# One inverse level of an RWKV-7 chunk solve moved from TensorE to VectorE, and the steps around it placed anew

## The chip, the cores and the metric

The kernel runs on one core of one Trainium2 chip, in float32 throughout. The metric is the device time of one execution in microseconds, the median of the runs.

## The reference, cut to what matters

One layer of a decoder: RMSNorm, an input projection, RWKV-7 time mixing (16 heads of 64) beside retention (8 heads of 128), an output projection, then a mixture of experts. There are 256 positions of a prompt and 8 short sequences of 8 positions ("the sample"), 320 positions in all. The change touches the RWKV part alone:

```python
def _wkv_step(S, inp):
    r, w, k, v, kk, b = inp
    sa = jnp.einsum('bhvk,bhk->bhv', S, -kk)
    S = S * w[:, :, None, :] + sa[..., :, None] * b[:, :, None, :] + v[..., :, None] * k[:, :, None, :]
    y = jnp.einsum('bhvk,bhk->bhv', S, r)
    return S, y
```

The kernel does not step through positions. It cuts the prompt into four chunks of 64 positions and solves each with matrices: Gram products of the scaled keys (b, k) with the queries (kk, r) give a strictly triangular 64x64 matrix M per head and chunk, and sa for all positions of a chunk follows from the inverse of 1 - M. That inverse is built by doubling: level 0 gives the inverse in blocks of 2, each further level k joins two blocks of size 2^k into one, X <- X + X (M masked to level k) X, up to level 5 (blocks of 64). The sample's matrix (blocks of 8) needs levels 0 to 2.

## The kernel before, in words

The projection weights come in tiles of 1 MB. For each of 8 pairs of RWKV heads (with one retention head beside it) there are seven tiles, in the order k, r, v, q, kr, vr, g. Each tile is a 2048x128 matrix multiplied with the 2048x320 activations by TensorE in 8 parts; a part is four matmul instructions with 320 columns as the trace counts them (line 722). The small work of a pair is cut into named steps. The tables PLAN (lines 71 to 79) and PLAN0 (for the first pair) list, for each tile, which steps follow each of its 8 parts; "|" ends a part, "@k" is the taking over of tile k's result, and a "-" marks a step of the pair before. Every engine walks the same list in order and does its own share of each step, so a step's place in the list is its place in the queue of TensorE, VectorE (DVE), ScalarE (ACT) and GpSimd (POOL) alike. Between engines only semaphores order the work. The first pair is written out, a loop runs over the other seven, and the last steps of the last pair run beside the output projection. Every VectorE instruction waits for the one before it; VectorE's are recorded at line 1432, ScalarE's at 1162, GpSimd's at 1984.

The steps that matter here:

- b2b (VectorE) makes the last operand for the Gram products. my copies the pair before's y out of PSUM; then mu (TensorE L866) sums it and va (L869) sums its squares; p2 is a product on VectorE for a later step.
- g0 to g3 are the Gram products of the four chunks (TensorE L754 and L755, results masked and evicted by VectorE), g4 those of the sample (L757, L758).
- "@v" on VectorE mixes v with its shifted self (three instructions); ScalarE copies the tile out of PSUM first. cv keeps v's last columns (two tiny copies).
- ax (ScalarE): packs the 32x32 diagonal blocks of M of the four chunks, two heads, into one tile Ac (four copies of 32 partitions, "ac"), and the off-diagonal ones for level 5 into A5 (two more).
- am (GpSimd): masks the sample's matrix for levels 1 and 2 (As), and Ac for levels 1 to 4 (Am).
- u0 (VectorE): level 0 of the prompt's inverse, as Vc = Ac * mask + unit; its 32x32 transposes (Uc); and Uc spread into a block-diagonal form (Ud).
- us0 (VectorE): level 0 of the sample's inverse and its transpose Us ("us").
- Level k of the prompt is three steps: k1 to k5 transpose Uc on TensorE (L785), i1 to i5 multiply with the mask of the level (eight small instructions, L795), j1 to j5 multiply both results (eight, L804); ScalarE and VectorE copy the results out between them, and VectorE adds and spreads again.
- zs1 (TensorE L777) and ds1 (L782) are level 1 of the sample, zs2 and ds2 level 2. zs1 needs As and Us.
- r0 to r3, a0 to a3 and s0 to s3 then step through the chunks; VectorE copies r2's result of the pair before early in tile k.

Before the change the order from tile v on was: g4 after part 4 of v; mu and g0 after part 5; g1; g2 and g3 after part 7; then after the parts of q: va, u0 | cv, us0 | | k1, i1 | zs1 | j1, pd | ds1 | k2, i2.

After the pairs come the output projection, a router and the experts, whose 400 MB of weights keep the DMA engines busy until the end.

Of the kernel before, what the change touches and what calls it, by code (L numbers as in the profile page):

```python
# [6 lines left out]
ALU = mybir.AluOpType  # L7
# [3 lines left out]
P = 128  # L11
# [8 lines left out]
NC = TP // C  # L20
NCH = NC + 1
LEVELS = 6
BK, NB32 = 32, 4
INNER = 5
# [82 lines left out]
def build_program(nc, xT, win, w_out, params, lora_mu, shT, lora_w, gmix, cst, head_cst,  # L107
# [3 lines left out]
    with ctx:  # L111
# [34 lines left out]
        ones = sbt(128)  # L146
# [36 lines left out]
        def cut(at, n, **axes):  # L183

            x = inv[:, at:at + n]
            return x.rearrange("p (c n) -> p c n", **axes) if axes else x
# [15 lines left out]
        Vc = cut(3712, 128, c=NC)  # L202
        squares = [x[:, 0:4 * T] for x in (GM.rearrange("p c n -> p (c n)"), tok.rearrange("p a c n -> p (a c n)"), wide4)]
# [89 lines left out]
        def sem(name):  # L293
            if name not in sems:
                sems[name] = ctx.enter_context(nc.semaphore(name))
            return sems[name]
# [22 lines left out]
        def wait_freed(e, step, p):  # L319

            e.wait_ge(free(step), nth(step, p))
# [10 lines left out]
        def done(name):  # L332

            return sem("done_" + name)

        def wait_done(e, name, p):
            e.wait_ge(done(name), p + 1)
# [338 lines left out]
        def _(pe):  # L676
# [11 lines left out]
            pe.wait_ge(sem("ones_set"), 1)  # L688
# [37 lines left out]
            def step(p, s):  # L726
# [43 lines left out]
                elif s in ("zs1", "zs2"):  # L770
                    k = int(s[-1])
                    pe.wait_ge(lmk, (INNER + 1) * p + k)
# [10 lines left out]
                elif s[0] == "k":  # L783
                    pe.wait_ge(inverse, 2 * (INNER * p + int(s[1])) - 1)
                    nc.tensor.transpose(b[:, 0:P], Uc[:, :, :], ident).then_inc(full(s), 1)  # L785
                elif s[0] == "i":
                    k = int(s[1])
                    pe.wait_ge(inverse, 2 * (INNER * p + k))
                    if k < INNER:
                        pe.wait_ge(lmk, (INNER + 1) * p + 2 + k)  # L790
                    else:
                        pe.wait_ge(done("ac"), 2 * p + 2)
# [364 lines left out]
        def _(act):  # L1157
# [62 lines left out]
            def step(p, s):  # L1220
# [33 lines left out]
                elif s == "ax":  # L1254
                    wait_freed(act, "g2", p)
                    wait_freed(act, "g3", p)
                    for q in range(NB32):
                        last = A(Ac[quarter[q], :, :], gcell[quarter[q], :, q % 2, :], ACT.Copy)
                    last.then_inc(done("ac"), 1)
                    for h in range(2):  # L1260
                        last = A(A5[quarter[2 * h], :, :], gcell[quarter[2 * h], :, 1, :], ACT.Copy)
                    last.then_inc(done("ac"), 1)
                elif s in ("k1", "k2", "k3", "k4"):
# [161 lines left out]
        def _(dve):  # L1425
# [23 lines left out]
            swapped = [i ^ 1 for i in range(32)]  # L1449

            FILL(eps[:, 0:1], NORM_EPS)
            FILL(eps[:, 1:2], LNX_EPS).then_inc(sem("eps_set"), 1)
            FILL(ones, 1.0).then_inc(sem("ones_set"), 1)
# [99 lines left out]
            def step(p, s):  # L1553
# [63 lines left out]
                elif s == "u0":  # L1617
                    dve.wait_ge(done("ac"), 2 * p + 1)
                    TT(Vc[:, :, :], Ac[:, :, :], inner[0][:, None, :].broadcast_to([P, NC, BK]), ALU.mult)
                    TT(Vc[:, :, :], Vc[:, :, :], unit[:, None, :].broadcast_to([P, NC, BK]), ALU.add)  # L1620
                    TR(Uc.rearrange("p c j -> p (c j)"), Vc.rearrange("p c j -> p (c j)")).then_inc(inverse, 1)
# [5 lines left out]
                elif s in ("i1", "i2", "i3", "i4"):  # L1627
                    wait_filled(dve, s, p)
                    spread(Zd, bank(s)[:, 0:P].rearrange("p (b j) -> p b j", b=NB32)).then_inc(free(s), 1)
                elif s in ("j1", "j2", "j3", "j4"):  # L1630
# [348 lines left out]
        def _(pool):  # L1979
# [16 lines left out]
            def step(p, s):  # L1996
                if s == "am":
                    wait_freed(pool, "g4", p)
                    for k in range(1, 3):
                        TT(As[:, k - 1, :], GM[:, NC, 0:P], lvlT[k], ALU.mult).then_inc(lmk, 1)  # L2000
                    pool.wait_ge(done("ac"), 2 * p + 1)
                    for k in range(1, INNER):
                        TT(Am[:, k - 1, :, :], Ac[:, :, :], inner[k][:, None, :].broadcast_to([P, NC, BK]), ALU.mult).then_inc(lmk, 1)
# [157 lines left out]
```

## Time and profile before

| | us |
|---|---|
| median of 3 runs | 1880.41 (1880.20 to 1882.89) |
| profiled execution, its own time | 1880.75 |
| span of that execution | 1878.9 |
| TensorE busy in the span | 1549.3 (82%) |
| VectorE busy | 627.8 (33%) |
| ScalarE busy | 275.0 (15%) |
| GpSimd busy | 62.0 (3%) |
| mean granted TensorE clock | 0.911 |

The span runs from the first to the last instruction; the execution's own time has what lies around it as well. The eight pairs take roughly the first half of the span; in it TensorE is busy in nearly every slice and the DMA engines in a third. In the second half it is the other way round: the experts' weights arrive at about 428 GB/s and TensorE waits for them. The mean clock is below 1 because of the second half; in the first it is at its upper level throughout.

### The profile page before, as it was taken

To read this page: it belongs to the slowest core of one execution; us is meant where nothing else is said; L and a number is where in the kernel's file an instruction comes from. 1 tells how busy PE (TensorE), PEld (TensorE's weight loads), DVE (VectorE), ACT (ScalarE), POOL (GpSimd) and SP (SyncE) were. 2 spreads that over 40 slices of the span, in tenths; PEclk is the share of its full clock that TensorE was granted. 3 is DMA by queue.
4 is the path that set the end of the run, shared out by engine and by line. 5 is a ranking of instruction groups with operands and counts; after the bars stand their busy time and mean duration, and the time that the engine had idled before them with its cause. 6 is when DMAs were issued, how large, how long until landed. Compare 5 with 4: busy or idle time off the path is not lost.

```text
span 1878.9 us, 24721 instructions
## 1 busy us (share of the span) xinstructions
PE 1549.3 (82%) x8990; PEld 891.2 (47%) x8990; DVE 627.8 (33%) x1264; ACT 275.0 (15%) x592; POOL 62.0 (3%) x103
## 2 busy tenths in 40 slices
PE   7999999999999999999996675766757667576664
PEld 4676767676767676766662231222312223122111
DVE  6746565656565656420031110111102111020014
ACT  2222222222222222200102000000000000000002
POOL 1000000000000000000000000000000000000000
PEclk9999999999999999999997887878878788787778
DMA  7323232323232323275489999999999999999996
GB/s 283 107 98 108 101 104 100 108 94 113 89 120 83 120 82 120 71 292 203 157 373 426 428 429 428 428 428 429 428 429 428 428 429 428 428 428 429 428 407 252
DMA packets 71904, 510.35 MB, mean 272 GB/s; under 512 B 20496, under 2 KB 23696, under 8 KB 37808
## 3 DMA queue, kind: packets, MB, share of 16 engines
q1 hardware_dynamic: 71808, 509.60, 67.1%
q8 instruction: 29, 0.48, 0.1%
q14 instruction: 19, 0.16, 0.0%
q0 software_dynamic: 48, 0.12, 0.0%
HBM read 499.87 MB, written 9.82 MB: 271 GB/s over the span
## 4 chain that ended last, share of the span: by engine, by line
PE 51%; DMA 34%; DVE 10%; issue 2%; SPq 1%; DVEq 1%; ACT 0%; ACTq 0%
DMA arena<-w_up 22%; PE ps_PJ L722 18%; DMA arena<-w_down 12%; DVE arena L1432 10%; PE ps_C L1079 8%; PE ps_PJ L933 7%; SPq L559 1%; PE ps_C L1130 1%; PE ps_SB L1130 1%; PE ps_YB L1130 1%; PE ps_C L795 1%; PE ps_RT L1130 1%; PE ps_SB L764 1%; PE ps_C L804 1%; PE ps_C L755 1%
## 5 line engine op out<-in xcount | busy, mean ns | idle before, releaser
L722 PE MATMUL ps_PJ<-arena 128*128 128x320 f32 x1792 | 539.8, 437 | 0.0
L1079 PE MATMUL ps_C<-arena 128*32 128x512 f32 x2048 | 286.5, 722 | 178.5 <-DMA arena<-w_gate 112.2
L722 PEld LDWEIGHTS ps_PJ<-arena 128*128 128x128 f32 x1792 | 322.8, 190 | 120.1 <-issue 18.0
L1432 DVE TENSOR_TENSOR arena<-arena,ps_PJ 128x512 f32<-128x512 f32 (+2 forms) x112 | 73.6, 657 | 612.7 <-PE ps_PJ L1033 493.3
L1079 PEld LDWEIGHTS ps_C<-arena 128*32 128x32 f32 x2048 | 79.8, 130 | 378.3 <-issue 375.9
L1432 DVE TENSOR_TENSOR arena<-arena 128x512 f32<-128x512 f32 (+12 forms) x311 | 161.8, 520 | 62.4 <-ACTq L421 26.7
L1162 ACT ACTIVATE arena<-ps_C 128x128 f32<-128x128 f32 (+3 forms) x68 | 27.5, 404 | 919.4 <-PE ps_C L1079 532.4
L933 PE MATMUL ps_PJ<-arena 128*128 128x320 f32 x512 | 142.4, 433 | 1.0 <-DVEq L421 1.0
L1162 ACT ACTIVATE arena<-arena 128x320 f32<-128x320 f32 (+11 forms) x206 | 98.0, 476 | 271.7 <-DVEq L421 87.6
L933 PEld LDWEIGHTS ps_PJ<-arena 128*128 128x128 f32 x512 | 95.5, 190 | 40.2 <-issue 3.3
L1432 DVE TENSOR_TENSOR arena<-ps_PJ,arena 128x512 f32<-128x512 f32 x32 | 22.1, 692 | 257.8 <-PE ps_PJ L1026 257.6
L1130 PE MATMUL ps_C<-arena 128*32 128x512 f32 x224 | 41.4, 818 | 79.3 <-DMA arena<-w_down 78.3
L1033 PE MATMUL ps_PJ<-arena 128*128 128x512 f32 (+1 forms) x192 | 96.4, 621 | 3.5 <-ACTq L421 3.3
L1026 PEld LDWEIGHTS ps_PJ<-arena 128*128 128x128 f32 x768 | 87.0, 192 | 12.6 <-issue 12.6
L1026 PE MATMUL ps_PJ<-arena 128*128 128x128 f32 x768 | 89.9, 277 | 0.0
L1984 POOL TENSOR_TENSOR arena<-arena 128x128 f32<-128x128 f32 (+2 forms) x80 | 55.7, 696 | 703.4 <-DVEq L421 380.5
L1432 DVE SCALAR_TENSOR_TENSOR arena<-arena 128x320 f32<-128x320 f32 (+6 forms) x145 | 72.6, 501 | 15.5 <-DVE arena L1432 10.9
L1033 PEld LDWEIGHTS ps_PJ<-arena 128*128 128x128 f32 (+1 forms) x192 | 26.6, 170 | 72.7 <-DVEq L421 45.4
L1432 DVE TENSOR_TENSOR arena<-ps_C,arena 128x320 f32<-128x320 f32 (+3 forms) x77 | 43.2, 561 | 49.7 <-PE ps_C L795 22.7
L1432 DVE RECIPROCAL arena<-arena 128x320 f32<-128x320 f32 (+1 forms) x29 | 54.6, 1881 | 6.0 <-ACTq L421 2.6
L1162 ACT ACTIVATE arena<-ps_SB 128x512 f32<-128x512 f32 (+4 forms) x80 | 36.4, 455 | 123.9 <-PE ps_SB L764 48.3
L1130 PEld LDWEIGHTS ps_C<-arena 128*32 128x32 f32 x224 | 7.0, 125 | 95.3 <-issue 95.3
(185 smaller groups left out, 1190.8 us busy)
## 6 DMA issues: line engine op xcount, KB each, us to landing
arena<-w_down SPq DMA_DIRECT2D x64, 2048.0 KB, 20.8
arena<-w_gate SPq DMA_DIRECT2D x61, 2048.0 KB, 20.6
arena<-w_up SPq DMA_DIRECT2D x61, 2048.0 KB, 20.3
arena<-win SPq DMA_DIRECT2D x59, 1024.0 KB, 4.8
arena<-w_out SPq DMA_DIRECT2D x16, 1024.0 KB, 7.5
arena<-w_gate SPq DMA_DIRECT2D x6, 1024.0 KB, 8.0
arena<-xT SPq DMA_DIRECT2D x8, 640.0 KB, 8.5
arena<-s_ret SPq DMA_DIRECT2D x8, 512.0 KB, 3.8
```

Of the source, the lines that this page charges most:

```text
L559: sp.dma_start(dst, src).then_inc(ex_in[s], 16)
L722: last = mm(pj(j)[:, 0:T], wt[j % NSLOT][:, kt, :], hT[:, kt, :], start=kt == 0, stop=kt == KT - 1)
L755: mm(b[:, 2 * C:320], Kd_[:, c, :], AR[:, c, 0:192], start=True, stop=True).then_inc(full(s), 1)
L764: last = nc.tensor.transpose(b[:, c * P:(c + 1) * P], src[:, c, :], ident)
L933: last = mm(pj(m)[:, 0:T], w[:, i, :], yT[:, KORD[i], :], start=i == 0, stop=i == KT - 1)
L1026: last = mm(XB[b][:, k * P:(k + 1) * P], x1[:, t, kt * P:(kt + 1) * P], pick[:, t, :], start=t == 0, stop=t == 2)
L1033: mm(XB[b][0:nt, :], gT[:, t0:t0 + nt], yp[:, n * F:(n + 1) * F], start=True, stop=True).then_inc(x_full[b], 1)
L1079: last = mm((GB, UB)[u][h * CAP:(h + 1) * CAP, :], xg[:, kt, h * CAP:(h + 1) * CAP], w[h](k), start=kt == 0, stop=kt == KT - 1)
L1130: last = mm(DB[n][h * CAP:(h + 1) * CAP, :], hhT[:, 2 * k + j, h * CAP:(h + 1) * CAP], w[h][:, j, n * F:(n + 1) * F], start=k + j == 0, st ...
L1162: ins = nc.scalar.activation(*args, **kw)
L1432: ins = build(*args)
L1984: ins = nc.gpsimd.tensor_tensor(*args)
```

## The change

Level 1 of the prompt's inverse is no longer done with k1, i1 and j1. u0 does it on VectorE: with blocks of 2 already inverted, one entry of a row and two columns of a group of four are all that changes, so two shuffles across partitions bring the rows needed into place and five small element-wise steps finish the level, ahead of the transposes. GpSimd makes the level's mask product Am[0] first for it. The four copies of ax that fill Ac are shared: two stay on ScalarE, two go to VectorE at the head of u0, and GpSimd waits for all four before any of its products. The Gram products move back by one part (g4 to part 5 of v, beside mu; g3 to the first part of q), p2 goes ahead of g4, cv ahead of ax and u0, and va stands behind cv. zs1, ds1 and the levels from 2 on keep their places. The banks of PSUM lose the three names, and the counts of the semaphores follow. The two semaphores of the set-up constants become one.

```diff
-    "C0": ["g0", "g3", "i1", "i2", "i3", "i4", "i5", "r0", "r1", "r2", "r3"],
+    "C0": ["g0", "g3", "i2", "i3", "i4", "i5", "r0", "r1", "r2", "r3"],
...
 PLAN = {
     "k": "-@g -u1 -th | -s1 | zw -u2 | -r2 -mr za | pc | -a2 pe | -mg | -s2",
     "r": "@k ck | -r3 | sq p1 | -a3 b1k ss | b1l | ps -s3 | pk | b1 b2a",
-    "v": "@r b2b cr -e3 | | | -my | g4 p2 | -mu g0 | g1 | g2 g3",
-    "q": "@v ax am -va u0 | cv us0 | | k1 i1 | zs1 | j1 pd | ds1 | k2 i2",
+    "v": "@r b2b cr -e3 | | | -my | p2 | g4 -mu | g0 | g1 g2",
+    "q": "@v g3 cv -va | ax am u0 | us0 | | zs1 | pd | ds1 | k2 i2",
...
 PLAN0 = {
-    "v": "@r b2b cr | | mk | | g4 p2 | g0 | g1 | g2 g3",
+    "v": "@r b2b cr | | mk | | g4 p2 | g0 | g1 | g2",
...
+        rows4, pair4 = cut(3584, 128, c=NC), inv[:, 1536:1600].rearrange("p (g e) -> p g e", e=2)
...
                 elif s in ("zs1", "zs2"):
-                    pe.wait_ge(lmk, (INNER + 1) * p + k)
+                    pe.wait_ge(lmk, (INNER + 1) * p + 1 + k)
...
                 elif s == "ax":
                     wait_freed(act, "g2", p)
                     wait_freed(act, "g3", p)
-                    for q in range(NB32):
+                    for q in range(2):
                         last = A(Ac[quarter[q], :, :], gcell[quarter[q], :, q % 2, :], ACT.Copy)
-                    last.then_inc(done("ac"), 1)
+                    last.then_inc(done("packing"), 1)
...
+            third_row = [i // 4 * 4 + 2 for i in range(32)]
+            second_row = [i // 4 * 4 + (1 if i % 4 == 0 else 2) for i in range(32)]
...
                 elif s == "u0":
-                    dve.wait_ge(done("ac"), 2 * p + 1)
+                    CP(Ac[quarter[2], :, :], gcell[quarter[2], :, 0, :])
+                    last = CP(Ac[quarter[3], :, :], gcell[quarter[3], :, 1, :])
+                    dve.wait_ge(done("packing"), 2 * p + 1)
+                    last.then_inc(done("ac"), 1)
                     TT(Vc[:, :, :], Ac[:, :, :], inner[0][:, None, :].broadcast_to([P, NC, BK]), ALU.mult)
                     TT(Vc[:, :, :], Vc[:, :, :], unit[:, None, :].broadcast_to([P, NC, BK]), ALU.add)
+                    x1, v1, sx = by_four(Am[:, 0, :, :]), by_four(Vc), by_four(rows4)
+                    SHUF(rows4[:, :, :], Vc[:, :, :], third_row)
+                    dve.wait_ge(lmk, (INNER + 1) * p + 1)
+                    TT(pair4[:, :, 0:1], x1[:, :, 2:3], sx[:, :, 3:4], ALU.mult)
+                    TT(x1[:, :, 3:4], x1[:, :, 3:4], pair4[:, :, 0:1], ALU.add)
+                    SHUF(rows4[:, :, :], Am[:, 0, :, :], second_row)
+                    TT(pair4[:, :, :], sx[:, :, 2:4], v1[:, :, 1:2].broadcast_to([P, BK, 2]), ALU.mult)
+                    TT(x1[:, :, 2:4], x1[:, :, 2:4], pair4[:, :, :], ALU.add)
+                    TT(Vc[:, :, :], Vc[:, :, :], Am[:, 0, :, :], ALU.add)
                     TR(Uc.rearrange("p c j -> p (c j)"), Vc.rearrange("p c j -> p (c j)")).then_inc(inverse, 1)
                     spread(Ud, Uc).then_inc(inverse, 1)
...
                 if s == "am":
                     wait_freed(pool, "g4", p)
+                    wait_done(pool, "ac", p)
+                    TT(Am[:, 0, :, :], Ac[:, :, :], inner[1][:, None, :].broadcast_to([P, NC, BK]), ALU.mult).then_inc(lmk, 1)
                     for k in range(1, 3):
                         TT(As[:, k - 1, :], GM[:, NC, 0:P], lvlT[k], ALU.mult).then_inc(lmk, 1)
-                    pool.wait_ge(done("ac"), 2 * p + 1)
-                    for k in range(1, INNER):
+                    for k in range(2, INNER):
                         TT(Am[:, k - 1, :, :], Ac[:, :, :], inner[k][:, None, :].broadcast_to([P, NC, BK]), ALU.mult).then_inc(lmk, 1)
```

Of the "for h in range(2)" copies into A5 on ScalarE nothing changes but the name of the semaphore.

## Rows read from the trace of the kernel before

**Rows 1.** The page: busy time, share of the span, instruction count.
```profile
PE 1549.3 (82%) x8990; PEld 891.2 (47%) x8990; DVE 627.8 (33%) x1264; ACT 275.0 (15%) x592; POOL 62.0 (3%) x103
```

**Rows 2.** Stretch of one pair: us, busy (count) by engine, PEclk, DMA share, GB/s.
```profile
432.90:526.20 93.30, 92.51 (x517) 65.46 (x516) 55.01 (x115) 23.50 (x56) 6.96 (x10) 1.00 0.30 102
```

**Rows 3.** Waits, 160 to 850 us, TensorE's weight loads: total us, times, longest.
```profile
PEld ps_SB L777 <- DVEq L421: 3.3, 7, 0.5
```

**Rows 4.** Timeline, TensorE, Gram stretch: start, us, instruction, count [idle before <-releaser].
```profile
427.56 7.70 PE L722 MATMUL ps_PJ<-arena 128*128 128x320 f32 x28
435.87 0.56 PE L757 MATMUL ps_SB<-arena 128*128 128x192 f32 x2 [0.60 <-DVEq L421]
...
436.59 1.24 PE L722 MATMUL ps_PJ<-arena 128*128 128x320 f32 x4
437.86 0.78 PE L866 MATMUL ps_RT<-arena 128*128 128x320 f32 x2
```

**Rows 5.** Timeline, VectorE, start of its chain and the Gram stretch.
```profile
412.43 0.29 DVE L1432 COPY arena<-ps_C 128x128 f32<-128x128 f32 x1 [1.56 <-PE ps_C L816]
...
437.05 0.49 DVE L1432 COPY arena<-ps_YB 128x320 f32<-128x320 f32 x1
...
443.18 0.49 DVE L1432 TENSOR_TENSOR arena<-ps_C,arena 128x320 f32<-128x320 f32 x1 [0.22 <-PE ps_C L755]
```

**Rows 6.** Timeline, TensorE, the first inverse level.
```profile
447.66 0.27 PE L785 MATMUL ps_C<-arena 128*128 128x128 f32 x1
...
448.35 1.34 PE L722 MATMUL ps_PJ<-arena 128*128 128x320 f32 x4
449.67 0.49 PE L777 MATMUL ps_SB<-arena 128*128 128x128 f32 x2
...
451.16 0.43 PE L804 MATMUL ps_C<-arena 128*32 128x128 f32 x8
451.52 1.34 PE L722 MATMUL ps_PJ<-arena 128*128 128x320 f32 x4
452.70 0.38 PE L782 MATMUL ps_SB<-arena 128*128 128x128 f32 x2
```

**Rows 7.** Timeline, VectorE, from the v mix to the sample's inverse.
```profile
444.08 0.40 DVE L1432 TENSOR_SCALAR arena<-arena 128x329 f32<-128x329 f32 x1 [0.41 <-DVE arena L1432]
...
445.65 0.85 DVE L1432 TENSOR_TENSOR arena<-arena 128x128 f32<-128x128 f32 x2 [0.23 <-DVE arena L1432]
...
448.58 0.62 DVE L1432 TENSOR_TENSOR arena<-arena 128x128 f32<-128x128 f32 x2
449.24 0.32 DVE L1432 STREAM_TRANSPOSE arena<-arena 128x128 f32<-128x128 f32 x1
```

**Rows 8.** Timeline, ScalarE, the six packing copies.
```profile
443.76 2.12 ACT L1162 ACTIVATE arena<-arena 32x128 f32<-32x128 f32 x6 [0.77 <-DVEq L421]
```

**Rows 9.** VectorE by form, whole span: busy, mean ns | idle before.
```profile
L1432 DVE STREAM_SHUFFLE arena<-arena 128x320 f32<-128x320 f32 x16 | 8.2, 515 | 0.2
...
L1432 DVE TENSOR_TENSOR arena<-arena 128x32 f32<-128x32 f32 x19 | 3.7, 193 | 0.6
...
L1432 DVE TENSOR_TENSOR arena<-ps_RT,arena 128x64 f32<-128x64 f32 x8 | 1.8, 225 | 0.3
...
L1432 DVE COPY arena<-arena 128x128 f32<-128x128 f32 x1 | 0.2, 226 | 0.0
```

**Rows 10.** Timeline, GpSimd, beside it.
```profile
445.91 0.45 POOL L1984 TENSOR_TENSOR arena<-arena 128x128 f32<-128x128 f32 x1 [0.18 <-POOL arena L1984]
```

**Rows 11.** Stretches around idle TensorE: columns as in rows 2.
```profile
59.90:67.00 7.10, 5.03 (x25) 4.06 (x25) 6.14 (x19) 0.00 (x0) 0.00 (x0) 1.00 0.00 0
1001.00:1003.40 2.40, 0.00 (x0) 0.00 (x0) 2.08 (x4) 0.00 (x0) 0.00 (x0) 1.00 1.01 430
1003.50:1006.90 3.40, 1.85 (x7) 1.34 (x7) 0.69 (x2) 1.04 (x2) 0.00 (x0) 0.50 1.02 434
1047.00:1051.20 4.20, 4.15 (x20) 1.13 (x24) 0.00 (x0) 0.00 (x0) 0.00 (x0) 0.50 1.02 429
```

More of the change, by code:

```diff
@@ L687, in _ @@
             last.then_inc(used, 1)
-            pe.wait_ge(sem("ones_set"), 1)
+            pe.wait_ge(sem("eps_set"), 2)
             pe.wait_ge(win_in[1], 16)
@@ L783, in step @@
                 elif s[0] == "k":
-                    pe.wait_ge(inverse, 2 * (INNER * p + int(s[1])) - 1)
+                    pe.wait_ge(inverse, 2 * ((INNER - 1) * p + int(s[1]) - 1) - 1)
                     nc.tensor.transpose(b[:, 0:P], Uc[:, :, :], ident).then_inc(full(s), 1)
@@ L787, in step @@
                     k = int(s[1])
-                    pe.wait_ge(inverse, 2 * (INNER * p + k))
+                    pe.wait_ge(inverse, 2 * ((INNER - 1) * p + k - 1))
                     if k < INNER:
@@ L791, in step @@
                     else:
-                        pe.wait_ge(done("ac"), 2 * p + 2)
+                        pe.wait_ge(done("packing"), 2 * p + 2)
                     for c in range(NC):
@@ L1256, in step @@
                     wait_freed(act, "g3", p)
-                    for q in range(NB32):
+                    for q in range(2):
                         last = A(Ac[quarter[q], :, :], gcell[quarter[q], :, q % 2, :], ACT.Copy)
-                    last.then_inc(done("ac"), 1)
+                    last.then_inc(done("packing"), 1)
                     for h in range(2):
                         last = A(A5[quarter[2 * h], :, :], gcell[quarter[2 * h], :, 1, :], ACT.Copy)
-                    last.then_inc(done("ac"), 1)
-                elif s in ("k1", "k2", "k3", "k4"):
+                    last.then_inc(done("packing"), 1)
+                elif s in ("k2", "k3", "k4"):
                     wait_filled(act, s, p)
@@ L1449, in _, with by_four @@
             swapped = [i ^ 1 for i in range(32)]
+            third_row = [i // 4 * 4 + 2 for i in range(32)]
+            second_row = [i // 4 * 4 + (1 if i % 4 == 0 else 2) for i in range(32)]
+            def by_four(x):
+                return x.rearrange("p c (g e) -> p (c g) e", e=4)
             FILL(eps[:, 0:1], NORM_EPS)
             FILL(eps[:, 1:2], LNX_EPS).then_inc(sem("eps_set"), 1)
-            FILL(ones, 1.0).then_inc(sem("ones_set"), 1)
+            FILL(ones, 1.0).then_inc(sem("eps_set"), 1)
             dve.nop().then_inc(proj_free, NL)
@@ L1626, in step @@
                     TR(Us, V[:, NC, :]).then_inc(done("us"), 1)
-                elif s in ("i1", "i2", "i3", "i4"):
+                elif s in ("i2", "i3", "i4"):
                     wait_filled(dve, s, p)
                     spread(Zd, bank(s)[:, 0:P].rearrange("p (b j) -> p b j", b=NB32)).then_inc(free(s), 1)
-                elif s in ("j1", "j2", "j3", "j4"):
+                elif s in ("j2", "j3", "j4"):
                     wait_filled(dve, s, p)
```

4 rows, old and new, of the table BANKS are left out of this document.

## The prediction

> **What bounds the kernel now.** I read the page first: TensorE is busy 82% of the span [rows 1], which says little, since stages with different limits are mixed in it. The view by stretch shows one pair of heads: every 93.3 us TensorE is busy 92.5 us at a granted clock of 1.00 (the upper level, 2.4 GHz), VectorE 55 us, the DMA engines 30% [rows 2]. So in the eight pairs a microsecond more or less on TensorE's own path is a microsecond of the kernel, while VectorE's busy share proves nothing: what counts is whether it is late at a point where TensorE waits. The waits of the weight loads name such a point: zs1, the first product of the sample's own inverse (L777), waited for VectorE in seven of seven pairs after the first, up to 0.5 us [rows 3]. The timelines give the other two. After b2b, g4 starts at 435.87, where 28 products of 0.27 us from 427.56 would have let it start at 435.12: 0.75 us late. Then mu is 0.19 late (436.59 and four products make 437.67, it starts at 437.86), because y's copy on VectorE runs from 437.05 to 437.54 [rows 4, 5]. That chain of VectorE hangs on the copy of r2 at 412.43, for which VectorE waited 1.56 us on TensorE [rows 5]; from there to y's copy it has no wait for TensorE above 0.1 us in its timeline. All numbers are of the pair that runs from 432.9 us; the others repeat it within 0.1 us.
>
> **Level 1 leaves TensorE.** k1 and i1 (a transpose, eight small products) stand between 447.66 and 448.35: 0.69. The four projection products after them reach zs1 at 449.67, 1.32 later, where they need 1.08: 0.24 more, part of it zs1's wait. So 0.93 goes before zs1. j1 costs 0.09 before it (449.99 to 451.16 for four products, 449.99 being zs1's 0.32 after 449.67), 0.36 itself and 0.10 after it (451.52 to 452.70): 0.55 goes behind zs1 [rows 6]. If nobody were late, that would be 1.48 us a pair, 11.8 us in all.
>
> **g4 and mu.** g4 goes one projection part (1.08) later, to 436.20, and mu directly behind it. The wait at g4 (0.75) ends, but mu is now reached at 436.92 and y's copy still ends at 437.54: nothing in the k and r tiles changes, the r2 copy is still released by TensorE, and "my" stands ahead of p2 and g4 as before ahead of g4. So mu starts at 437.86 as before and waits 0.94 = 0.75 + 0.19. With g4 and the same projection parts done at that moment, the gain is 0. If the anchor moved earlier, it would be at most 0.94 a pair (7.5 us); if the swap of p2 and g4 slowed mu's own chain, some tenths the other way. I take 0.
>
> From mu on TensorE does the same work in another order: g3 moves behind the first q part, beside va. It is at the point of the old k1 (447.66) within 0.02, then makes one more part of 1.08: it reaches zs1 at 448.76.
>
> **VectorE up to zs1.** It must finish u0 and then us0 (Us), in this order, before zs1. Before: the last Gram product was evicted by 443.67 (443.18 + 0.49), the mix of v, u0, cv and us0 followed, and Us was ready at 449.56 (449.24 + 0.32), 0.11 before zs1 started [rows 5, 6, 7]. There is no slack there. Now the same chain:
> - The last eviction ahead of v's mix is g2's; with g3 gone from this place TensorE is 0.55 (one Gram pair) earlier, so it ends at 443.13. The mix keeps its 1.76 (443.67 to 445.43): 444.89.
> - g3 is evicted now behind it, 0.22 + 0.49 as in its row: 445.60. cv moves ahead of u0, 0.27 + 0.47: 446.34. Both were in the chain before, so up to here only 0.54 of the order is gained and 0.71 given back.
> - Two packing copies. The nearest copy takes 0.23 [rows 9]; with gaps 0.63: 446.97. ScalarE's other two of the six that took 2.12 [rows 8] start when g3 is evicted and need 0.7, so they are done before. Sharing the copies takes 1.4 us off ScalarE's part and puts 0.6 on the chain.
> - u0's old content: 445.43 to the end of its spread at 447.69, 2.26 [rows 7]: 449.23.
> - Its new content: two shuffles, two products and sums of 32 columns, two of 64, one of 128, and a wait for GpSimd's Am1. A shuffle of 320 columns takes 0.515, one of 128 then 0.31 (about 1 ns a column, as between the products of 64 and 32), with mask load and gap 0.37; twice 0.74. 32 columns 0.193 twice; 64 columns 0.225 twice; 128 columns 0.29; five gaps of 0.03; the wait 0.2 as other waits of this chain [rows 7, 9]. Sum 2.22: 451.45.
> - us0's 1.13 (448.43 to 449.56): 452.58. u0's seven two-input steps (two old, five new) run beside GpSimd's six products (Am1 comes first now, the rest follow): two such steps took 0.85 beside GpSimd and 0.62 without it [rows 7, 10]; I add 0.1. Us at 452.7, zs1 at 452.8.
>
> TensorE reaches zs1 at 448.76 and waits 4.0 us. Against 449.67 zs1 is 3.1 late; behind it 0.55 of j1 is saved. **A pair becomes 2.58 us longer.** In pair 0 VectorE is late already (it builds masks there), zs1 hangs on the same chain, and I take 2.4. Sum: 7 x 2.58 + 2.4 = 20.4 us. Nothing gives it back: the whole later part of the pair is shifted, VectorE waits for TensorE at r2 in the next pair, and the output projection and the expert loads begin when TensorE has come so far. Bounds: with every step at its shortest and no gap for the wait zs1 is 0.5 earlier, 17 us in sum (it could not go below nothing: nine steps are added and none taken out); with every two-input step slowed as the pair in rows 7 and 0.3 at each of two waits 0.6 later, 25 us. The respaced i2 to k5 keep their places; the banks C0 to C2 lose one use each; SP's queue issues the same pieces in the same order, and nothing new is queued there.
>
> Two waits are added. VectorE waits for ScalarE's two copies ahead of u0, with us0 behind it: free, as worked out. GpSimd now waits for "ac" before the two masks of the sample (As) too, which zs1 also needs: "ac" comes at 447.0, and three products of 0.45 and their gaps of 0.18 [rows 10] end at 449, before Us; it costs nothing while Us is later, and zs1 would start at 449.1 if VectorE were done.
>
> The Trainium skill ("SBUF — State Buffer", section "Who interferes with whom") says that a VectorE instruction with two SBUF inputs contends with a GpSimd instruction that reads SBUF, and that the one that comes second is blocked for the whole of the other. The 0.85 against 0.62 agrees in sign; by full blocks of 0.45, six of them, a pair would be 2.7 longer still, 22 us in all. The rows show a quarter of that, and I stay with them.
>
> **The clock.** In the pairs it never left 1.00: in pair 0 TensorE stood 2.07 us before g4 (60.0 to 62.1), and the stretch around it is at 1.00. But where it stood from 1001.0 to 1003.9 the clock was 1.00 until 1003.4 and 0.50 (1.2 GHz) in the stretch behind; and when dense work came back at 1047 it ran at 0.50 for 4.2 us, half of which, 2.1, is lost [rows 11]. A wait of 4.0 us once a pair is longer than the one that was followed by a fall and longer than any in the pairs now. In how many of the eight pairs the clock falls the rows don't say: none costs 0, all cost 8 x 2.1 = 17. I take four: 8.4 us.
>
> The Trainium skill ("TensorE: Matmul & The Clock Gate", section "What's actually happening") speaks against the change here: "the default state is throttled, and activity releases the throttle". By that rule all eight pairs would restart at the lower level, and the sum would be 1918.
>
> **Forecast**: on the profiled execution's 1880.75 (span 1878.9 and 1.85 around it) 20.4 + 8.4 make 1909.5; the median of the runs is 0.3 lower, 1909.
>
> **Rivals.**
> - A: the wait comes, the clock holds. For it: 4.0 us stands among 92 us of dense work, and 2.07 did nothing. Time 1880.4 + 20.4 = 1901.
> - B: GpSimd's products and VectorE's block one another fully (from rows, every two-input step as long as the 0.45 product beside it: six times 0.45 a pair), with some clock falls: 1880.4 + 20.4 + 22 + 8 = 1931. Against it: the pair of 0.85.
> - C, faster: VectorE's chain isn't what zs1 waits for, because the copies, shuffles and small steps fall into time in which VectorE idles now (0.9 us before g2's eviction, 0.4 before the mix). Then level 1 pays its 1.48 a pair: 1880.4 - 11.8 = 1868.6. It decides at 0.55: if Us comes less than 0.55 us later than now the pair is shorter, else longer. Against it: the added steps are nine and the smallest such step in the rows takes 0.19, so 1.7 at least, and rows 3 show no slack.
> - D: the pieces balance within 4 us of 1880; it needs the same as C with half the cover.
>
> **Chances.** Forecast (the wait and clock falls in two pairs or more) 0.50, A 0.34, B 0.04, C 0.08, D 0.04. Range: the likeliest and A with their bounds, 1880.4 + 17 - 2 (pair 0 may cost less) to 1880.4 + 25 + 17: 1895 to 1922; above and below it lie B, C, D. No change means within 0.2% (3.8 us), about what a measurement of this kernel can tell: slower 0.88, same 0.04, faster 0.08.
>
> **What will show it.** On the changed kernel's timeline: zs1's weight load waits some 4 us for VectorE in each pair (3 or less would make my VectorE sum wrong, none would make C right); g4 has no wait and mu one of 0.9; the period is 95.9 us plus the clock's share; from the end of the eviction ahead of v's mix to Us it takes 9.6 us (443.13 to 452.7; before 5.9, 443.67 to 449.56); there are stretches at 0.50 in the pairs, none before. The forecast is wrong if the period is below 93.3, or if the clock's share is 0 or above 17 us.

## The result, and the profile after

The changed kernel takes 1919.7 us (median of 5 runs, 1917.9 to 1920.5) against 1880.4: a ratio of 1.0204 (95% interval 1.0193 to 1.0215), slower. The profiled execution took 1919.68 us by its own time.

Its page: the span, TensorE's busy time, and the costliest group of instructions.

```profile
span 1917.9 us, 24456 instructions
...
PE 1559.5 (81%) x8854; PEld 902.9 (47%) x8854; DVE 633.2 (33%) x1328; ACT 267.5 (14%) x568; POOL 60.1 (3%) x103
...
L723 PE MATMUL ps_PJ<-arena 128*128 128x320 f32 x1792 | 552.4, 447 | 0.0
```

TensorE has fewer instructions (8854 against 8990) and is yet busy longer (1559.5 us against 1549.3 in [rows 1]): the 1792 projection products (L723 now, L722 before) take 447 ns each in the records; in the kernel before, the same group had 437. They run slower, and nothing about them was changed.

The stretch of one pair (columns as in [rows 2]) and the waits of TensorE from 60 to 900 us (total, times, longest), which answer to [rows 2, 3]:

```profile
374.80:473.60 98.80, 93.98 (x500) 67.22 (x499) 55.74 (x123) 22.50 (x53) 6.69 (x10) 0.97 0.28 96
```

```profile
PE ps_SB L778 <- DVEq L422: 31.3, 8, 3.9
PE ps_RT L867 <- DVEq L1717: 5.4, 7, 0.9
```

A pair takes 98.8 us here and its clock is 0.97, where it was 93.3 and 1.00. zs1 (L778 now) waits 3.9 us in each of the seven pairs after the first and 3.7 in the first; mu (L867) waits for y's copy in the seven pairs that have one; the wait at g4 is gone but for pair 0.

TensorE's timeline of the same pair, answering to [rows 4, 6]: the products ahead of g4, g4, mu, the four parts ahead of zs1, zs1, and what follows it.

```profile
447.38 8.78 PE L723 MATMUL ps_PJ<-arena 128*128 128x320 f32 x32
455.99 0.49 PE L758 MATMUL ps_SB<-arena 128*128 128x192 f32 x2
456.32 0.49 PE L759 MATMUL ps_SB<-arena 128*128 128x192 f32 x2
457.57 0.78 PE L867 MATMUL ps_RT<-arena 128*128 128x320 f32 x2 [0.76 <-DVEq L1717]
...
464.14 4.47 PE L723 MATMUL ps_PJ<-arena 128*128 128x320 f32 x16
472.56 0.80 PE L778 MATMUL ps_SB<-arena 128*128 128x128 f32 x2 [3.95 <-DVEq L422]
473.15 4.47 PE L723 MATMUL ps_PJ<-arena 128*128 128x320 f32 x8
477.42 0.63 PE L783 MATMUL ps_SB<-arena 128*128 128x128 f32 x2
477.85 1.71 PE L723 MATMUL ps_PJ<-arena 128*128 128x320 f32 x4
```

g4 starts without a wait; mu starts 1.25 after g4's second half, 0.94 later than it could; zs1 starts 14.99 us after mu (forecast 14.94). Then look at the durations: sixteen products of a projection take 4.47 ahead of zs1, and eight take 4.47 behind it.

VectorE's timeline, answering to [rows 5, 7]: the copy of r2, y's copy, the evictions of g1 and g2 (one line), g3's, cv with the two packing copies, and u0 and us0 to the transpose that ends in Us; behind it ScalarE's four copies (two into Ac, two into A5).

```profile
432.23 0.29 DVE L1433 COPY arena<-ps_C 128x128 f32<-128x128 f32 x1 [1.56 <-PE ps_C L817]
...
456.76 0.49 DVE L1433 COPY arena<-ps_YB 128x320 f32<-128x320 f32 x1
...
461.63 1.13 DVE L1433 TENSOR_TENSOR arena<-ps_C,arena 128x320 f32<-128x320 f32 x2 [1.13 <-PE ps_C L756]
...
464.74 0.49 DVE L1433 TENSOR_TENSOR arena<-ps_C,arena 128x320 f32<-128x320 f32 x1 [0.22 <-DVE arena L1433]
465.50 1.09 DVE L1433 COPY arena<-arena 128x1 f32 x4 [0.27 <-DVE arena L1433]
466.84 0.75 DVE L1433 TENSOR_TENSOR arena<-arena 128x128 f32<-128x128 f32 x2 [0.25 <-ACTq L422]
...
467.64 0.30 DVE L1433 STREAM_SHUFFLE arena<-arena 128x128 f32<-128x128 f32 x1
468.08 0.70 DVE L1433 TENSOR_TENSOR arena<-arena 128x32 f32<-128x32 f32 x2
...
469.15 0.99 DVE L1433 TENSOR_TENSOR arena<-arena 128x64 f32<-128x64 f32 x3
...
470.64 1.46 DVE L1433 TENSOR_TENSOR arena<-arena 128x512 f32<-128x512 f32 x3
472.14 0.31 DVE L1433 STREAM_TRANSPOSE arena<-arena 128x128 f32<-128x128 f32 x1
```

```profile
465.32 1.43 ACT L1163 ACTIVATE arena<-arena 32x128 f32<-32x128 f32 x4 [0.45 <-DVEq L422]
```

From the end of g2's eviction (462.76) to Us (472.45) it is 9.69 us; the forecast said 9.6.

The stretches around zs1's wait, by window (columns as in [rows 2]; the granted clock, third from the end, is the point):

```profile
468.70:472.40 3.70, 0.00 (x0) 0.00 (x0) 3.16 (x11) 0.00 (x0) 1.39 (x4) 0.94 0.70 222
472.60:479.20 6.60, 6.60 (x16) 4.62 (x17) 0.60 (x2) 1.59 (x4) 0.00 (x0) 0.53 0.00 0
479.50:486.00 6.50, 6.50 (x46) 4.01 (x45) 4.29 (x11) 1.28 (x4) 0.00 (x0) 1.00 0.46 161
```

TensorE does nothing for 3.7 us of this stretch, and shortly before it starts again the clock goes to 0.50 (1.2 GHz); it works through 6.6 us of the shifted pair at a mean of 0.53 and is back at 1.00. The clock's records have nine such falls in the pairs of this execution, one in each of the later seven and two in pair 0 (one behind each of its two stops), four of them 3.4 us long and five 6.8, 47.6 us in all. In the profiled execution of the kernel before there was none, though the first of pair 0's two stops (2.07 us ahead of g4) is in it as well.

### The profile page after: what moved, and what is told of

The parts are those of the page before. It is cut to its first block, busy times and chain, and to the rows that moved or that the text cites. A ratio compares the mean times of both kernels' runs of the same rounds, so it can differ in the third digit from the quotient of the medians.

```text
span 1917.9 us, 24456 instructions
## 1 busy us (share of the span) xinstructions
PE 1559.5 (81%) x8854; PEld 902.9 (47%) x8854; DVE 633.2 (33%) x1328; ACT 267.5 (14%) x568; POOL 60.1 (3%) x103
## 4 chain that ended last, share of the span: by engine, by line
PE 47%; DMA 34%; DVE 13%; issue 3%; SPq 1%; ACT 1%; DVEq 1%; ACTq 0%
DMA arena<-w_up 22%; PE ps_PJ L723 16%; DVE arena L1433 13%; DMA arena<-w_down 12%; PE ps_C L1080 8%; PE ps_PJ L934 7%; SPq L560 1%; PE ps_C L1131 1%; PE ps_SB L1131 1%; ACT arena L1163 1%; PE ps_YB L1131 1%; PE ps_RT L1131 1%; PE ps_SB L765 1%; PE ps_C L796 1%; PE ps_SB L778 0%
## 5 line engine op out<-in xcount | busy, mean ns | idle before, releaser
L723 PE MATMUL ps_PJ<-arena 128*128 128x320 f32 x1792 | 552.4, 447 | 0.0
L723 PEld LDWEIGHTS ps_PJ<-arena 128*128 128x128 f32 x1792 | 334.7, 196 | 127.2 <-issue 24.0
L1433 DVE TENSOR_TENSOR arena<-arena 128x320 f32<-128x320 f32 (+13 forms) x343 | 168.1, 490 | 62.7 <-ACTq L422 27.9
L934 PE MATMUL ps_PJ<-arena 128*128 128x320 f32 x512 | 142.4, 433 | 1.0 <-DVEq L422 1.0
L1163 ACT ACTIVATE arena<-arena 32x128 f32<-32x128 f32 (+12 forms) x190 | 92.8, 489 | 265.2 <-DVEq L422 84.3
L934 PEld LDWEIGHTS ps_PJ<-arena 128*128 128x128 f32 x512 | 95.5, 190 | 40.2 <-issue 3.3
L1027 PEld LDWEIGHTS ps_PJ<-arena 128*128 128x128 f32 x768 | 87.0, 192 | 12.6 <-issue 12.6
L1433 DVE TENSOR_TENSOR arena<-ps_C,arena 128x320 f32<-128x320 f32 (+3 forms) x69 | 37.6, 545 | 51.6 <-PE ps_C L796 24.3
```

The source lines that it names most:

```text
L723: last = mm(pj(j)[:, 0:T], wt[j % NSLOT][:, kt, :], hT[:, kt, :], start=kt == 0, stop=kt == KT - 1)
L934: last = mm(pj(m)[:, 0:T], w[:, i, :], yT[:, KORD[i], :], start=i == 0, stop=i == KT - 1)
L1027: last = mm(XB[b][:, k * P:(k + 1) * P], x1[:, t, kt * P:(kt + 1) * P], pick[:, t, :], start=t == 0, stop=t == 2)
L1163: ins = nc.scalar.activation(*args, **kw)
L1433: ins = build(*args)
```

## The experiments

Each is timed against the kernel before on the same chip. Ratios are to it. Two of them edit the kernel before (the Gram products' part alone; mu one part later in the kernel before), the others the changed kernel. Each kernel has one profiled execution; what is said of waits and falls is of that one.

### The Gram products' part alone

```diff
-    "v": "@r b2b cr -e3 | | | -my | g4 p2 | -mu g0 | g1 | g2 g3",
+    "v": "@r b2b cr -e3 | | | -my | p2 | g4 -mu g0 | g1 | g2 g3",
```

> The kernel before with one edit: g4 one projection part later, beside mu, and p2 ahead of it; level 1 stays on TensorE and g0 to g3 keep their places. My theory (mu hangs on y's copy on VectorE): the 0.75 us wait at g4 goes and comes back at mu, mu waits 0.9 us, the pair stays at 93.3 us and the time at 1880 (within 1 us). Rival (the wait at g4 was a loss of its own): 0.75 a pair is gained, 1880.4 - 6 = 1874.

Measured: 1880.5 us, ratio 0.9999 (0.9990 to 1.0008). TensorE's waits, 160 to 800 us:

```profile
PE ps_RT L866 <- DVEq L1697: 5.2, 6, 0.9
```

The wait left g4 and stands at mu, 0.87 us a time, and zs1 follows zs1 by 93.30 us as before. Moving a step out of a wait gains nothing when the step behind it waits for the same chain.

### Level 1 on VectorE with the old Gram order

```diff
-    "v": "@r b2b cr -e3 | | | -my | p2 | g4 -mu | g0 | g1 g2",
-    "q": "@v g3 cv -va | ax am u0 | us0 | | zs1 | pd | ds1 | k2 i2",
+    "v": "@r b2b cr -e3 | | | -my | g4 p2 | -mu g0 | g1 | g2 g3",
+    "q": "@v ax am -va u0 | cv us0 | | | zs1 | pd | ds1 | k2 i2",
...
```

> The changed kernel with the Gram order of the kernel before (g4 p2 | mu g0 | g1 | g2 g3, then ax, va, u0, cv, us0); level 1 on VectorE as changed. My theory (the loss is VectorE's chain up to Us, and the clock that falls after the wait): the chain from the last Gram eviction to Us loses g3's 0.71 and starts 0.54 later, so zs1 comes 15 us after mu as in the changed kernel, it waits 3.9 us, the clock falls in every pair: 1918 to 1920. Rival (the order of the Gram products behind v's mix costs the time): the time falls back by 0.7 a pair or more, 1914 or less.

Measured: 1915.7 us (1914.1 to 1917.8), ratio 1.018 (1.0165 to 1.0196). TensorE's waits, 160 to 800 us:

```profile
PE ps_SB L778 <- DVEq L422: 27.1, 7, 3.9
PE ps_SB L758 <- DVEq L422: 3.6, 7, 0.6
```

zs1 waits 3.9 us as in the changed kernel, and starts 14.91 us after mu. So the order of the Gram products has no part in the wait. The median is 4 us below the changed kernel's, between my figure and the rival's. The profiled executions differ by 1.9 (1917.8 and 1919.7), and the falls account for most of that: four long and four short ones here (40.8 us at 0.50), five long and four short there (47.6), and a pair with a long fall is about 1.5 us longer than one with a short fall (98.8 against 97.3). Whether the medians' other 2 us are falls too is not shown.

### The wait filled with products that nobody reads

The products write to a PSUM bank whose content has been evicted; the outputs don't depend on them.

```diff
                     if k == 1:
+                        wait_freed(pe, "g1", p)
+                        for _ in range(7):
+                            mm(psum["C1"][:, 0:T], ident, hT[:, 0, :], start=True, stop=True)
                         pe.wait_ge(done("us"), 2 * p + 1)
```

> The changed kernel with seven products of 320 columns on TensorE (0.54 us each, 3.8 us in all, into a PSUM bank whose content is used up; nothing reads them) ahead of zs1's wait for Us. VectorE's chain is untouched. My theory (two parts: 20.5 us of wait net of what level 1 gave back, and 18 us because the clock falls after each wait): no stretch at 0.50 in the pairs, the pair's period 95.9 us, 1880.4 + 20.5 = 1901. Rival (the clock has no share and the chain costs it all): unchanged, 1919.7. Rival (the load of TensorE itself pulls the clock down): stretches at 0.50 remain, 1910 or more.

Measured: 1900.7 us (1899.8 to 1901.4), ratio 1.0105 (1.0089 to 1.0120). One pair by window:

```profile
366.30:462.20 95.90, 94.88 (x514) 67.98 (x514) 55.71 (x123) 22.55 (x53) 6.67 (x10) 1.00 0.29 99
```

The clock is 1.00 throughout, the pair takes 95.9 us, and 19 us have gone that no change to VectorE's chain took away. This separates the loss: 20 us are the wait net of what level 1 gave back, the other 19 are the clock. In the changed kernel, from its second pair on, it takes 98.6 to 98.95 us from one zs1 to the next where the fall between them is long, 97.3 and 97.6 where it is short: against 95.9, a long fall costs 2.7 to 3.0 us and a short one 1.4 or 1.7. TensorE executes 3.8 us more work a pair and the kernel is faster for it.

### Four and two such products

The same edit with 4 and with 2 in place of 7.

> As the kernel with the filled wait, but with four such products (2.2 us) ahead of zs1, so TensorE stands still some 1.8 us a pair. In the kernel before it stood 2.07 us once in pair 0 and the clock held. If that length is harmless: no stretch at 0.50 in the pairs and 1901 as with the full filling. If any stop of such a length lowers the clock: falls in some pairs, 1.35 to 3.0 us each as measured in the changed kernel, 1905 to 1919.

> As the kernel with the filled wait, but with two products of 0.54 us ahead of zs1: TensorE stands still 2.9 us a pair. With four products it stood 1.8 us and the clock held in all pairs after the first; with none it stood 3.9 us and the clock fell in all. Theory (the length of the stop decides, and 2.96 us was followed by a fall in the kernel before): falls in most pairs, 1905 to 1918. Rival (only the longest stops matter): no fall, 1901.

Measured: with four, 1901.3 us (ratio 1.0106, 1.0090 to 1.0121); with two, 1912.9 us (1910.5 to 1917.8; ratio 1.0177, 1.0161 to 1.0192). The waits at zs1 and the clock, first with four, then with two products:

```profile
PE ps_SB L781 <- DVEq L422: 14.0, 8, 1.8
```

```profile
160.00:800.00 640.00, 622.20 (x3417) 445.26 (x3415) 368.03 (x819) 153.21 (x359) 46.90 (x70) 1.00 0.28 97
```

```profile
PE ps_SB L781 <- DVEq L422: 23.0, 8, 2.9
```

```profile
196.00:560.00 364.00, 349.98 (x1906) 252.32 (x1905) 213.18 (x468) 86.15 (x201) 26.79 (x40) 1.00 0.29 100
560.00:800.00 240.00, 231.57 (x1269) 164.65 (x1270) 133.00 (x294) 54.63 (x130) 17.24 (x24) 0.96 0.25 89
```

A stop of 1.8 us a pair costs its length and nothing more: the clock is 1.00 from 160 to 800 us. A stop of 2.9 us is followed by a fall in four of eight pairs (pair 0 and the last three: 0.96 from 560 us on) and by none in the four between (1.00 from 196 to 560), though the eight stops are alike within 0.06 us. That is one execution, the fastest of the four. So the length alone does not decide near 3 us; at 3.7 to 3.9 us all eight fell in the changed kernel. What tells the four from the others I can't show: but for pair 0 they differ in the moment at which they come, not in the work around them.

Nor does it decide at 2.07 us. Pair 0's stop ahead of g4 is in all 14 kernels of this case, before, changed and the twelve experiments, at 2.07 or 2.08 us and behind the same 9.85 us of products. In nine of the 14 profiled executions a fall of 3.4 us follows it, in five none does, the kernel before among these. With g4 alone moved, whose pair 0 is that of the kernel before, it does:

```profile
62.90:66.30 3.40, 3.40 (x10) 2.60 (x9) 3.09 (x10) 0.00 (x0) 0.00 (x0) 0.50 0.00 0
```

### All four packing copies on ScalarE

```diff
                 elif s == "ax":
-                    for q in range(2):
+                    for q in range(NB32):
...
                 elif s == "u0":
-                    CP(Ac[quarter[2], :, :], gcell[quarter[2], :, 0, :])
-                    last = CP(Ac[quarter[3], :, :], gcell[quarter[3], :, 1, :])
...
```

> The changed kernel with all four packing copies into Ac on ScalarE again, none on VectorE; the two into A5 follow. ScalarE starts them when g3 is evicted (465.32 in the pair read) and takes 0.36 each, so u0's first product starts at 466.8 to 466.9, where it started at 466.84 with shared copies, because VectorE has cv's two tiny copies to do meanwhile. My theory: nothing, 1919.7 within 1.5 us. Rival (the two copies on VectorE are 0.6 us of the chain, as my sum put them): 0.6 a pair earlier, 1915. Rival (sharing did shorten the packing by 0.7): 0.7 a pair later, 1925.

Measured: 1918.6 us (1915.2 to 1920.9), ratio 1.0198 (1.0184 to 1.0212): no difference from the changed kernel. VectorE's timeline from g3's eviction to u0's first product:

```profile
465.08 0.49 DVE L1433 TENSOR_TENSOR arena<-ps_C,arena 128x320 f32<-128x320 f32 x1 [0.22 <-DVE arena L1433]
465.84 0.47 DVE L1433 COPY arena<-arena 128x1 f32 x2 [0.27 <-DVE arena L1433]
467.08 0.76 DVE L1433 TENSOR_TENSOR arena<-arena 128x128 f32<-128x128 f32 x2 [0.77 <-ACTq L422]
```

u0 starts 1.51 us after g3's eviction (465.57 to 467.08); with shared copies it is 1.61 (465.23 to 466.84). VectorE waits 0.77 for ScalarE in place of copying for 0.6. So it is the same who makes the copies: taking both off the chain shortened it by 0.1, not by the 0.6 that they take on it.

### us0 ahead of u0

```diff
-        rows4, pair4 = cut(3584, 128, c=NC), ...
+        rows4, pair4 = cut(0, 128, c=NC), ...
-    "q": "@v g3 cv -va | ax am u0 | us0 | | zs1 | pd | ds1 | k2 i2",
+    "q": "@v g3 cv -va | us0 ax am u0 | | | zs1 | pd | ds1 | k2 i2",
```

> The changed kernel with us0 (the sample's own Us) ahead of ax and u0 on VectorE, in place of behind u0; the scratch rows of the shuffles lie in another place, since Us is live during u0. Nothing else moves. My theory (zs1 waits only for the chain in which us0 stands behind u0, and k2 stands late enough for u0): Us is ready before TensorE comes to zs1; zs1 waits 0.6 us for GpSimd's As, which stands behind the packing copies; no stretch at 0.50; a pair takes 92.5 us; 1874. Rival (the chain is late at k2 in the same way): k2 waits 2 us or more and the time stays above 1890.

Measured: 1874.8 us (1873.6 to 1876.5), ratio 0.9968 (0.9956 to 0.9980), 0.3% faster than before. zs1 in the timeline (TensorE):

```profile
446.00 0.48 PE L778 MATMUL ps_SB<-arena 128*128 128x128 f32 x2 [0.76 <-POOLq L422]
```

The same work, with one step in another place in VectorE's order, and 45 us are back. zs1 waits 0.76 for the mask that GpSimd makes behind the packing copies, as the second added wait of the prediction said (it gave 0.3 to 0.4 for it). No stretch of the pairs is at 0.50, a pair takes 92.7 us.

### GpSimd's products apart from u0

```diff
...
+                    for k in range(1, 3):
+                        TT(As[:, k - 1, :], ...)
                     wait_done(pool, "ac", p)
                     TT(Am[:, 0, :, :], ...)
-                    for k in range(1, 3):
-                        TT(As[:, k - 1, :], ...)
+                    pool.wait_ge(inverse, 2 * (INNER - 1) * p + 1)
                     for k in range(2, INNER):
```

> The changed kernel with GpSimd's products apart from u0: the two As masks first (before the packing is done), then Am for level 1, and Am for levels 2 to 4 only when VectorE has transposed Uc. So one GpSimd product in place of six runs beside u0's steps. The five new two-input steps and the two old ones took 2.44 us beside GpSimd where their durations alone would give 1.8. Theory: 0.6 us a pair less wait at zs1, 1915, if the clock falls as before. Rival (the two engines do not disturb one another here): 1919.7. Rival (each of the six blocks a step of VectorE for its whole 0.45): 2 us a pair or more, 1903 or less.

The counts for which TensorE and VectorE wait follow the new order of the masks.

Measured: 1923.9 us (1922.4 to 1924.6), ratio 1.0230 (1.0215 to 1.0246). Slower than the changed kernel, if by little (their intervals meet at 1.0215), which no theory had. VectorE's timeline of u0 and us0: two products of 128 columns, the steps of 32, those of 64 and 128, and the spread with us0's two:

```profile
466.68 0.92 DVE L1433 TENSOR_TENSOR arena<-arena 128x128 f32<-128x128 f32 x2 [0.25 <-ACTq L422]
...
468.08 0.47 DVE L1433 TENSOR_TENSOR arena<-arena 128x32 f32<-128x32 f32 x2
...
468.92 0.82 DVE L1433 TENSOR_TENSOR arena<-arena 128x64 f32<-128x64 f32 x3
...
470.23 1.77 DVE L1433 TENSOR_TENSOR arena<-arena 128x512 f32<-128x512 f32 x3
```

The steps of 32 columns went from 0.70 to 0.47 and those of 64 and 128 from 0.99 to 0.82, as expected. But the first two products went from 0.75 to 0.92, and the spread with us0's from 1.46 to 1.77. Beside the spread GpSimd's products are new. Beside the first two there was one already in the changed kernel; it started 0.06 behind VectorE's first there and took 0.55 itself; here it starts 0.01 ahead and takes 0.45, and VectorE's pair is what takes longer (GpSimd's timeline, the changed kernel, then this one):

```profile
466.90 0.55 POOL L2004 TENSOR_TENSOR arena<-arena 128x128 f32<-128x128 f32 x1 [16.20 <-DVEq L422]
```

```profile
466.67 0.45 POOL L2004 TENSOR_TENSOR arena<-arena 128x128 f32<-128x128 f32 x1 [6.67 <-DVEq L422]
```

zs1 starts 15.05 us after mu, as before (14.99). The sum of the disturbance is where it was. The stop at zs1 is 4.0 us. The profiled execution took 2.7 us more than the changed kernel's (1922.4 against 1919.7), and the falls account for nearly all of it: nine again, but 54.4 us long in place of 47.6, all of the later seven long. The stop hardly changed (by 0.07); what it cost afterwards did.

### us0 first, GpSimd apart, mu one part later

```diff
-    "v": "@r b2b cr -e3 | | | -my | p2 | g4 -mu | g0 | g1 g2",
+    "v": "@r b2b cr -e3 | | | -my | p2 | g4 | -mu g0 | g1 g2",
```

with the edits of the last two.

> The changed kernel with us0 ahead of ax and u0, GpSimd's products apart from u0 as in that experiment, and mu one projection part behind g4 (g4 | mu g0 | g1 g2, then g3). Theory: level 1's 1.48 us a pair is gained in full, and the 0.94 us for which mu waited for y's copy is filled with a projection part: 93.3 - 2.4 = 90.9 us a pair, clock 1.00 in all pairs, 1880.4 - 19.4 = 1861. Rival (VectorE's chain is then late at k2): some tenths to 2 us a pair of wait at k2, 1863 to 1877. Rival (the clock or the chain costs in another way): above 1880.

Measured: 1863.5 us (1862.9 to 1864.6), ratio 0.9907 (0.9891 to 0.9922). A pair takes 91.15 us, neither g4, mu nor zs1 waits; i2 waits 0.40.

### mu one part later in the kernel before

```diff
-    "v": "@r b2b cr -e3 | | | -my | g4 p2 | -mu g0 | g1 | g2 g3",
+    "v": "@r b2b cr -e3 | | | -my | p2 | g4 g0 | g1 -mu | g2 g3",
```

> The kernel before with the steps of tile v in another order alone: p2 | g4 g0 | g1 mu | g2 g3, so g4 is one part later and mu one part and a Gram product behind the point at which it had to wait for y's copy. Level 1 stays on TensorE. In the run with g4 alone moved the wait came back at mu, 0.87 us a pair. Theory (mu's wait is a wait for y's copy and nothing else): neither g4 nor mu waits, 0.94 a pair less, 92.4 us, 1880.4 - 7.5 = 1873. Rival (VectorE is then late at the Gram evictions or at zs1): less than half of it, 1877 or more.

Measured: 1878.0 us (1875.9 to 1879.6), ratio 0.9981 (0.9972 to 0.9990). The rival's case: TensorE's waits, 160 to 800 us,

```profile
PE ps_C L795 <- DVEq L421: 5.2, 7, 0.9
```

i1 now waits 0.7 us a pair for u0's Ud. mu's wait was covering for a chain on VectorE that is nearly as late. In the kernel with three edits, where level 1 has left TensorE, the later mu left no such wait; that it is because nothing there needs Ud before i2 is read from the plan, and no run moves mu alone in the changed kernel.

### What i2 waits for

In the kernel with three edits:

```diff
-                    pool.wait_ge(inverse, 2 * (INNER - 1) * p + 1)
                     for k in range(2, INNER):
+                        if k == 3:
+                            pool.wait_ge(inverse, 2 * (INNER - 1) * p + 1)
```

> As the kernel with all three edits, but GpSimd makes Am for level 2 directly behind Am for level 1; only those for levels 3 and 4 wait for Uc. There i2 waited 0.4 us a pair on TensorE and its weight load up to 0.9 us for GpSimd. Theory: this wait goes, 0.3 to 0.4 a pair, 1863.5 - 3 = 1860.5. Rival (Am for level 2 then runs beside u0's small steps and delays Ud by as much as it gains): 1863 or more.

Measured: 1864.7 us (1863.1 to 1865.4), ratio 0.9911 (0.9895 to 0.9926); no gain. GpSimd's product for level 3, VectorE's spread into Ud, and i2 on TensorE:

```profile
442.14 0.46 POOL L2004 TENSOR_TENSOR arena<-arena 128x128 f32<-128x128 f32 x1 [2.32 <-DVEq L422]
442.15 0.99 DVE L1433 TENSOR_TENSOR arena<-arena 128x512 f32<-128x512 f32 x1
...
443.44 0.42 PE L796 MATMUL ps_C<-arena 128*32 128x128 f32 x8 [0.40 <-DVEq L422]
```

The view of the weight loads gave GpSimd as the one waited for, 0.8 us. It was not: in this run Am for level 2 was there 3.6 us before i2, and nothing changed. i2 comes 0.3 after the end of the spread, and the spread takes 0.99 beside a GpSimd product where it takes 0.69 alone. So:

```diff
-                            pool.wait_ge(inverse, 2 * (INNER - 1) * p + 1)
+                            pool.wait_ge(inverse, 2 * (INNER - 1) * p + 2)
```

> As the kernel with Am for level 2 made early, but GpSimd starts Am for levels 3 and 4 only when VectorE has spread Ud, in place of when it has transposed Uc. In the run before the spread took 0.99 us beside a GpSimd product in place of 0.69, and i2 waited 0.40 for its end. Theory (that product lengthens the spread, and the spread is what i2 waits for): the spread takes 0.69, i2 waits 0.1, a pair is 0.3 shorter, 2.4 us in all: 1864.7 - 2.4 = 1862. Rival (i2 waits for something else): 1864.5.

Measured: 1861.3 us (1861.1 to 1864.5), ratio 0.9904 (0.9888 to 0.9921), the lowest median of all, though its interval holds the one of three edits as well. The spread and i2:

```profile
441.20 0.70 DVE L1433 TENSOR_TENSOR arena<-arena 128x512 f32<-128x512 f32 x1
...
442.19 0.43 PE L796 MATMUL ps_C<-arena 128*32 128x128 f32 x8
```

0.70 for the spread, less than 0.2 of wait at i2, 90.9 us a pair against 91.2: the 2.4 us a pair below the 93.3 of the kernel before are the sum of the level's 1.48 and mu's 0.94.

## Why the prediction was right, and where it was off

The direction, the wait at zs1 and the range came out. By the sign that the prediction set for itself one term did not: it called itself wrong if the clock's share was above 17 us, and the share is 19.

- **What bounds the kernel**: held. TensorE's path in the pairs carries every loss: 38.8 us of the 39.0 in the span are there when the last pair ends (844.25 against 805.41 for the first transposes behind it), and the experts' stage gives nothing back.
- **g4 and mu, gain 0**: held. mu starts 0.94 later than it could; the edit alone measured 0.9999.
- **TensorE at zs1, 4.0 us early**: held, 3.95 (3.66 in pair 0).
- **VectorE's chain to Us**: held as a sum, 9.69 against 9.6, and 14.99 against 14.94 from mu to zs1. By its parts: to the end of the packing copies 3.83 (462.76 to 466.59) against 3.84, from there to Us 5.86 against 5.73. The small steps took 0.70 and 0.99 beside GpSimd where their durations alone gave 0.42 and 0.80, for which the sum had only 0.1; that the old products took 0.75 and not 0.85, and that the wait for Am1 cost 0.1 and not 0.2, brought a little over half of that back. So the sum's closeness is in part luck.
- **A pair 2.58 longer, 20.4 in all**: held. With the wait filled a pair took 95.9 us (forecast 95.9) and the kernel 1900.7, rival A's 1901.
- **The clock**: that it would fall behind the new wait held, the term was mis-sized. I took four falls of 2.1 us, 8.4 in all; the filled wait puts it at 19 us. I had no row for how many pairs would have one and took half of them: it fell in eight pairs of eight, twice in pair 0. And the 2.1 came from a row that can't give it. [rows 11] has 4.2 us of work at 0.50 from 1047.0 on, but by then the clock had been down since 1040.9, during TensorE's stop from 1036.1 to 1047.0, so those 4.2 us are the last part of a fall of 10.2 (columns as in [rows 2]):

```profile
1036.20:1040.90 4.70, 0.00 (x0) 0.00 (x0) 0.00 (x0) 2.39 (x4) 0.00 (x0) 1.00 1.02 432
1041.00:1047.00 6.00, 0.00 (x0) 0.00 (x0) 0.00 (x0) 0.00 (x0) 0.00 (x0) 0.50 0.99 423
```

  Behind zs1 the clock falls when the stop is nearly over (at 471.9, zs1 at 472.56), and 6.2 us of work lie in a long fall: 2.7 to 3.0 are lost, 2.4 a pair in the mean of long and short. With eight falls at 2.1 the sum would have been 1918. That is what the Trainium skill's rule ("TensorE: Matmul & The Clock Gate", section "What's actually happening") gave, and it was the better guide than my halving of it. That the stop of 2.07 us in the rows had no fall behind it was chance: the same stop has one in nine of 14 executions.
- **GpSimd beside VectorE**: the Trainium skill ("SBUF — State Buffer", section "Who interferes with whom") has a VectorE instruction with two SBUF inputs blocked by a GpSimd one that reads SBUF. The traces agree in kind: the spread takes 0.99 with a GpSimd product beside it and 0.69 alone, two products of 128 columns 0.92 and 0.62. They don't show a block of the full 0.45 at each meeting: 0.3 was the most, and in the changed kernel all six together cost some 0.6 a pair. The chance of rival B was rightly small: by full blocks it would have been 22 us.
- **C and D**: refuted in this order of the steps. Not in another: with us0 ahead of u0 the same nine added steps no longer delay Us, and 0.6 of the level's 1.48 us a pair appears, with zs1 waiting 0.76 for GpSimd's mask.

The result lies 10.7 us above the forecast and inside the range, 2.3 below its upper end, and all of the distance is the clock's term. The upper end had 17 us for the clock and 25 for the wait; the clock went 2 beyond its part, and the result is inside because the wait came at its middle, 20.

## What to carry to other kernels

Before work is moved onto an engine that is a third busy, look for the one point at which the bound engine waits for it: if the chain to that point has no slack now, each step put ahead of it is paid in full, and the cheapest repair is the order of the steps on the idle engine. And a stop of TensorE is to be priced with the clock behind it: here one of 1.8 us a pair cost its length, one of 3.9 us cost 2.4 us a pair more than its length.

## What was not expected of the hardware

- Stops of the same length (2.87 to 2.93 us) were followed by a fall of the clock in four pairs and not in the other four of one execution, and one and the same stop of 2.07 us in nine of 14 executions. The seven stops of 1.8 us in one execution never were, those of 3.7 to 4.0 us always.
- A fall in the pairs lasts 3.4 or 6.8 us, and which of the two it is differs from pair to pair: the profiled executions of level 1 with the old Gram order and of GpSimd apart differ by 4.6 us (1917.8 and 1922.4) with waits at zs1 that are the same within 0.15. Between their later zs1 steps three of six pairs took 97.2 to 97.5 us in the one, and all six 98.6 to 99.0 in the other.
- A VectorE product of 512 columns takes 0.69 us alone and 0.99 with one GpSimd product of 0.45 in it. Moving GpSimd's products away from some steps put the same delay on others.
- A wait on several semaphores was put down to GpSimd by the view of the waits, 3.6 us after GpSimd had been done; the timeline of the producers told what it was.
